# A two-layer encoder with a routed expert stage: the first block's rows picked in turned form, its pass unrolled ahead of the block count

## The chip, the cores and the metric

The kernel runs on one core of a Trainium2 chip. The engines named below are TensorE (PE; its weight loads are listed as PEld), VectorE (DVE), ScalarE (ACT), GpSimd (POOL) and SyncE (SP). The metric is the device time of one execution in microseconds (us).

## What is computed

Two layers over 768 tokens (a sequence of 512 and one of 256) of width 1024, in float32. Each layer has a mixer, an attention to a memory of 256 rows per sequence, and an expert stage. Cut to what matters here:

```python
def memory_cross_attention(x, mem, wq, wkv, wo):     # 4 heads of 256
    q = x @ wq; k, v = split(mem @ wkv)
    return softmax(q @ k.T / 16) @ v @ wo

def grouped_moe(x, router_w, router_bias, w_gate, w_up, w_down):
    e_idx, gw = route(x, router_w, router_bias)      # 2 of 16 experts for each token
    # tokens sorted by expert, each expert's list padded to blocks of 128
    for each block b, expert e:
        h = silu(xb @ w_gate[e]) * (xb @ w_up[e])    # 128 x 512
        yb = h @ w_down[e]                           # 128 x 1024
    y[token] = sum over its 2 slots of gw * yp[slot]

def trunk(x, mem, weights):
    for l in range(2):
        x = layer_norm(ALPHA * x + parallel_mixer(x, ...))
        x = layer_norm(ALPHA * x + memory_cross_attention(x, ...))
        x = layer_norm(ALPHA * x + grouped_moe(x, ...))
```

## The kernel before

Tokens lie in six chunks of 128 (`x[:, c, :]`). A product that must be exact to float32 is made of three faster ones: each operand is split into a high part (ScalarE copies it to the fast type: `split`, `high`, `split_part`) and a low part (VectorE subtracts: `low_weights`, `low`, `low_part`), and `three` (line 2078) multiplies high by high, high by low and low by high. Each engine's program is written out by hand in order; semaphores tie them.

**Memory attention.** Twelve items (a chunk and a pair of heads). For item i TensorE computes scores (`cross_scores`, L2362) two items ahead, ScalarE takes the exponential (L1147), VectorE normalises (`cross_norm`, L1691 and L1694), TensorE turns the result (`turn4`, L2094), ScalarE copies it back (L1164), and after every fourth item TensorE multiplies by the values (L2408). Between these stand the splits of the output weights wx0 to wx3. ScalarE splits wx1 in its turn i = 3, between the copy of item 2 and the exponential of item 4. VectorE's loop stands so: `cross_norm(i)`, `cross_max(i + 2)`, then `low_weights("wx1")` at i = 2.

**Router.** `ROUTER_ORDER` lists TensorE's work: `x3` turns a chunk, `rl` makes its logits (L2424), `rk` the ranks of tokens inside their experts (L2475 to L2480), `wx` output products of the attention, `b0` the first block. VectorE's `choose` finds the experts, `place` the slots and, for the first block, one-hot matrices `pick[c]` (L1794): row t of chunk c has a one in the column of its slot. `b0` multiplies `pick[c]` by the chunk, two products of 512 columns for each chunk (L2447), summed over six chunks in banks 5 and 6. ScalarE copies the two banks to `first_x` (L866), `turn_block(first_x)` turns them in eight transposes (L2493), ScalarE makes the high part (L1223), VectorE the low part (`low_block_xT(0)`, L1807).

**Block table.** After `place(2)` VectorE computes the table of blocks (L1844 to L1864): which expert each of 29 blocks belongs to, where its token list lies, and the number of blocks. The last copy (L1864) raises `ids_ready`. Every engine then reads the number of blocks (`value_load`) and enters its loop. GpSimd waits for `ids_ready` too before it loads the token list of block 1 (L782) and gathers its rows (L785).

**Expert block** (TensorE): gate products (24 of 512 columns, L2517), up products in two halves (L2527), two transposes of h (L2533, after VectorE's `hl_done`), the eight transposes of the next block's rows (`turn_block(xb)`, L2493, after the gather), two more of h (L2542), eight down products (L2553). VectorE multiplies h (L1922, L1924), makes the next rows' low part and the low parts of the next gate and up weights (`low_part`, L1802). Before its loop VectorE makes the low parts 0 to 3 of the first block's weights, finds every token's slots and weights (L1871 to L1902) and, in the first layer, the low part of the next layer's first weights (`low_weights("kvg")`, L1359).

```python
cross_norm(i)
if i + 2 < 12: cross_max(i + 2)
if i == 2: low_weights("wx1")
```

## Time and profile before

| | us |
|---|---|
| median of 3 runs | 2361.14 |
| lowest and highest | 2359.64, 2363.04 |
| the profiled execution | 2357.11 |
| its span, first to last instruction | 2355.3 |
| TensorE, VectorE, ScalarE, GpSimd busy | 2208.6, 1323.8, 992.5, 198.4 |
| mean granted clock of TensorE | 0.963 of full |

The profiled execution is 4.03 us below the median and 1.8 us above its span. The chain that ended last lies on TensorE for 79% of the span, on VectorE for 11% and on ScalarE for 6%. TensorE is the engine to keep fed: a change pays where TensorE stands idle or works at the lower of its two clocks, and hardly elsewhere.

### The profile page before, as it was taken

The page shows a single profiled execution, that of the slowest core. Times are in us where ns is not written, and L with a number is a line of the kernel's source. Part 1 is how long each engine was busy: PE and PEld are TensorE (multiplying, and loading weights), DVE is VectorE, ACT ScalarE, POOL GpSimd, SP SyncE. Part 2 cuts the span into 40 slices and gives each one's busy share as a digit, 9 for nine tenths or more (in the row PEclk, how much of TensorE's full clock was granted, in tenths as well). Part 3 has the DMA queues.
Part 4 walks back from the last instruction along what each step waited for, and adds up shares of the span by engine and source line. Part 5 has one row for each costly group of instructions (what it writes and reads, how often), then busy time and mean ns, then how long its engine had stood idle before and what let it go on. Part 6 is the DMA issues. An engine that isn't in the chain of part 4 may idle for free.

```text
span 2355.3 us, 35471 instructions
## 1 busy us (share of the span) xinstructions
PE 2208.6 (94%) x13292; PEld 1853.1 (79%) x13292; DVE 1323.8 (56%) x2101; ACT 992.5 (42%) x1648; POOL 198.4 (8%) x236
## 2 busy tenths in 40 slices
PE   8899988999999899999889989899999989999997
PEld 7788866989889677777687887598988877777774
DVE  2775377542244766556867636846214556656667
ACT  3354475123232355555235536622323224555553
POOL 0000011000000331000100000100000022200004
PEclk9899998999999899999899999999999989999999
DMA  4145111131110599999511112023211038999996
GB/s 154 45 162 175 37 72 55 55 110 70 55 45 28 192 377 372 382 376 359 199 50 36 37 36 90 10 82 108 86 41 55 37 146 303 378 378 375 383 377 223
DMA packets 78404, 385.64 MB, mean 164 GB/s; under 512 B 10456, under 2 KB 11848, under 8 KB 43464
## 3 DMA queue, kind: packets, MB, share of 16 engines
q1 hardware_dynamic: 55120, 327.83, 37.3%
q0 software_dynamic: 10096, 30.38, 3.6%
q10 hardware_dynamic: 13064, 25.75, 3.0%
q8 instruction: 81, 1.33, 0.2%
q14 instruction: 43, 0.35, 0.0%
HBM read 352.79 MB, written 46.07 MB: 169 GB/s over the span
## 4 chain that ended last, share of the span: by engine, by line
PE 79%; DVE 11%; ACT 6%; issue 2%; DMA 1%; POOL 0%; DVEq 0%; ACTq 0%; SPq 0%
PE bank L2078 39%; PE bank L2553 10%; PE bank L2527 9%; PE bank L2517 8%; PE bank L2228 2%; PE bank L2408 2%; PE bank L2094 2%; ACT x_transposed L1045 1%; PE bank L2362 1%; PE bank L2218 1%; PE bank L2245 1%; PE bank L2493 1%; DVE weight_slots_parts L1361 1%; ACT weight_slots_parts L904 1%; ACT scratch L1003 1%
## 5 line engine op out<-in xcount | busy, mean ns | idle before, releaser
L2078 PE MATMUL bank<-weight_slots_parts,x_transposed_parts 128*128 128x256 f32 x2496 | 475.8, 292 | 13.9 <-ACT mixer_region L968 13.9
L2078 PEld LDWEIGHTS bank<-weight_slots_parts,x_transposed_parts 128*128 128x128 f32 x2496 | 404.9, 200 | 15.2 <-ACT mixer_region L968 15.2
L1802 DVE TENSOR_TENSOR weight_slots_parts<-weight_slots,mixer_region_parts 128x2048 fp32r<-128x2048 f32 x140 | 321.5, 2315 | 85.9 <-ACT mixer_region_parts L1190 85.8
L1190 ACT ACTIVATE mixer_region_parts<-weight_slots 128x2048 fp32r<-128x2048 f32 x140 | 261.0, 1909 | 25.2 <-ACT x_transposed L1265 18.1
L2078 PE MATMUL bank<-x_transposed_parts,weight_slots_parts 128*128 128x512 f32 (+1 forms) x1024 | 263.9, 345 | 0.0
L1361 DVE TENSOR_TENSOR weight_slots_parts<-weight_slots,weight_slots_parts 128x2048 fp32r<-128x2048 f32 x58 | 132.9, 2292 | 231.5 <-ACT weight_slots_parts L904 231.0
L2553 PE MATMUL bank<-weight_slots,x_transposed 128*128 128x512 f32 x560 | 246.4, 593 | 0.0
L2527 PE MATMUL bank<-mixer_region_parts,x_transposed_parts 128*128 128x256 f32 x1120 | 207.3, 283 | 0.1
L2517 PE MATMUL bank<-mixer_region_parts,x_transposed_parts 128*128 128x512 f32 x560 | 194.3, 418 | 4.9 <-DVE x_transposed_parts L1807 4.9
L2078 PEld LDWEIGHTS bank<-x_transposed_parts,weight_slots_parts 128*128 128x128 f32 x1024 | 181.3, 194 | 22.3 <-issue 0.7
L2553 PEld LDWEIGHTS bank<-weight_slots,x_transposed 128*128 128x128 f32 x560 | 103.4, 190 | 117.9 <-issue 101.7
L2078 PE MATMUL bank<-weight_slots_parts,mixer_region_parts 128*128 128x256 f32 x1056 | 181.5, 291 | 4.8 <-DVE mixer_region_parts L1333 4.8
L2527 PEld LDWEIGHTS bank<-mixer_region_parts,x_transposed_parts 128*128 128x128 f32 x1120 | 176.9, 192 | 2.8 <-DVE weight_slots_parts L1802 1.5
L2078 PE MATMUL bank<-weight_slots_parts,x_parts 128*128 128x256 f32 x576 | 167.0, 290 | 0.0
L2078 PEld LDWEIGHTS bank<-weight_slots_parts,mixer_region_parts 128*128 128x128 f32 x1056 | 155.0, 200 | 5.4 <-DVE weight_slots_parts L1361 5.2
L2527 PE MATMUL bank<-weight_slots_parts,x_transposed_parts 128*128 128x256 f32 x560 | 158.4, 283 | 0.0
L2078 PE MATMUL bank<-mixer_region_parts,weight_slots_parts 128*128 128x512 f32 x512 | 137.3, 389 | 0.0
L2517 PEld LDWEIGHTS bank<-mixer_region_parts,x_transposed_parts 128*128 128x128 f32 x560 | 106.6, 190 | 35.2 <-issue 13.2
L904 ACT ACTIVATE weight_slots_parts<-weight_slots 128x2048 fp32r<-128x2048 f32 x58 | 111.0, 1914 | 53.9 <-DMA weight_slots<-in_wkv_mem 31.6
L2078 PEld LDWEIGHTS bank<-weight_slots_parts,x_parts 128*128 128x128 f32 x576 | 114.7, 199 | 0.0
L2078 PEld LDWEIGHTS bank<-mixer_region_parts,weight_slots_parts 128*128 128x128 f32 x512 | 96.0, 188 | 19.6
L2517 PE MATMUL bank<-weight_slots_parts,x_transposed_parts 128*128 128x512 f32 x280 | 110.7, 395 | 0.0
(308 smaller groups left out, 3605.0 us busy)
## 6 DMA issues: line engine op xcount, KB each, us to landing
weight_slots<-in_w_gate SPq DMA_DIRECT2D x70, 1024.0 KB, 7.3
weight_slots<-in_w_up SPq DMA_DIRECT2D x70, 1024.0 KB, 7.0
weight_slots<-in_w_down SPq DMA_DIRECT2D x70, 1024.0 KB, 8.0
weight_slots<-in_w_in SPq DMA_DIRECT2D x20, 1024.0 KB, 5.0
slots_y<-x_transposed ACTq DMA_DIRECT2D x66, 256.0 KB, 7.2
weight_slots<-in_wkv_mem SPq DMA_DIRECT2D x16, 1024.0 KB, 4.9
slots_y<-in_consts SPq DMA_DIRECT2D x6, 2304.0 KB, 17.8
weight_slots<-in_w_out SPq DMA_DIRECT2D x8, 1024.0 KB, 4.8
```

What stands on the lines that cost most here:

```text
L904: nc.scalar.activation(half_hi(name), half_raw(name), ACT.Copy).then_inc(w_hi, 1)
L1003: nc.scalar.activation(probs[:, j, 0:nk], probs[:, j, 0:nk], ACT.Exp, bias=st[:, 4 + j:5 + j], accum_out=st[:, 8 + j:9 + j])
L1190: nc.scalar.activation(hi, raw, ACT.Copy).then_inc(moe.high_ready, 1)
L1361: v.tensor_tensor(half_lo(name), half_raw(name), half_hi(name).bitcast(F32), ALU.subtract).then_inc(w_lo, 1)
L1802: v.tensor_tensor(lo, raw, hi.bitcast(F32), ALU.subtract).then_inc(moe.low_ready, 1)
L2078: ins = pe.matmul(ps, lhs[i](k), rhs[j](k), start=k == 0 and a == 0, stop=k == ks - 1 and a == 2)
L2094: ins = pe.transpose(ps[:, k * P:(k + 1) * P], source(k), ident)
L2228: done(pe.matmul(ps[:, 0:nb * P], qT[hp, j, c * P:(c + 1) * P], kT[hp, k0 * P:(k0 + nb) * P], start=True, stop=True), key)
L2408: ins = pe.matmul(ps[:, jj * 256:(jj + 1) * 256], vm[:, SEQ_OF[2 * cp] * MC + k, j * P:(j + 1) * P], xpt[:, j // 2, k, :], start=(k == 0), ...
L2517: ins = pe.matmul(banks[2][:, :], x_[:, 4 * h + k, :], w_[:, k, :], start=h == 0 and k == 0 and a == 0, stop=h == 1 and k == 3 and a == 2)
L2527: ins = pe.matmul(banks[bank][:, 0:256], x_[:, k, :], w_[:, k, :], start=k == 0 and a == 0, stop=k == KD - 1 and a == 2)
L2553: ins = pe.matmul(banks[5 + h][:, :], hbT[:, k, :], parts[4 + h][0][:, k, :], start=(k == 0), stop=(k == 3))
```

## The change

1. The first block's rows are formed already turned. `b0` now takes 128 columns of x as the stationary operand and `pick[c]` as the moving one: eight products of 128 columns for each chunk. Since eight groups of columns are summed in two banks, two products of zeros (one row, 512 columns) clear the banks first; GpSimd writes the row of zeros. The copies to `first_x` and its eight transposes are gone; ScalarE makes the high part out of the banks.
2. `b0` is spread otherwise in `ROUTER_ORDER`: chunks (0, 1), (2, 3), (4, 5) in place of (0, 1, 2), (3, 4), (5).
3. The first block's pass is written out ahead of the loop and of reading the block count on TensorE and VectorE. VectorE's `low_first_xT` stands in the middle of the block table; `low_part(2, 3)` stands behind the table; the slots and weights (L1871 to L1902) and `low_weights("kvg")` are spread over the first block or stand behind it.
4. `low_weights("wx1")` in the memory attention moves from i = 2 to i = 3.

```diff
-                ("x3", 4, 0), ("x3", 4, 1), ("rl", 1), ("rk", 0), ("wx", 5, 1), ("rk", 1), ("b0", (0, 1, 2)), ("x3", 5, 0), ("x3", 5, 1),
-                ("rl", 2), ("b0", (3, 4)), ("rk", 2), ("b0", (5,))])
+                ("x3", 4, 0), ("x3", 4, 1), ("rl", 1), ("rk", 0), ("wx", 5, 1), ("rk", 1), ("b0", (0, 1)), ("x3", 5, 0), ("x3", 5, 1),
+                ("rl", 2), ("b0", (2, 3)), ("rk", 2), ("b0", (4, 5))])
...
                         if c == 0:
-                            pool.wait_ge(moe.xT_filled, 2)
+                            tile_filled(pool, ("b0", 1))
...
                     for h in range(2):
-                        drain_copy(("b0", h), first_x[:, 512 * h:512 * h + 512], 512)
+                        tile_filled(act, ("b0", h))
+                        nc.scalar.activation(xbT_hi[:, 4 * h:4 * h + 4, :], bank_of(("b0", h))[:, :].rearrange("p (k t) -> p k t", k=4),
+                                             ACT.Copy).then_inc(moe.xT_high_ready, 1)
+                        own(moe.xT_high_ready)
-                    act.wait_ge(moe.xT_filled, 2)
-                    block_xT()
...
-                        if i == 2:
+                        if i == 3:
                             low_weights("wx1")
...
+                    def low_first_xT():
+                        for h in range(2):
+                            dve.wait_ge(moe.xT_high_ready, h + 1)
+                            v.tensor_tensor(xbT_lo[:, 4 * h:4 * h + 4, :], bank_of(("b0", h))[:, :].rearrange("p (k t) -> p k t", k=4),
+                                            xbT_hi[:, 4 * h:4 * h + 4, :].bitcast(F32),
+                                            ALU.subtract).then_inc((drain_sem(("b0", 0)), moe.xT_ready)[h], 1)
...
                     low_part(1, 2)
-                    low_part(2, 3)
                     choose(2)
                     place(2)
...
                     v.tensor_reduce(r_be, cmp_, AX.X, ALU.add)
+                    low_first_xT()
...
                     v.tensor_copy(r_nbi, r_end[:, NE - 1:NE]).then_inc(ids_ready, 1)
-                    low_block_xT(0)
+                    low_part(2, 3)
                     low_part(3, 4)
...
                         v.tensor_tensor(hb[:, 0:256], gact[:, 0:256], banks[3][:, 0:256], ALU.mult).then_inc(moe.hl_done, 1)
+                        if first:
+                            own_weights()
...
+                            if first:
+                                routed_weights(0)
                             low_block_xT(b + 1)
+                            if first:
+                                routed_weights(1)
                             low_part(0, 4 * b + 5)
+                            if first:
+                                late_slots()
                             low_part(1, 4 * b + 6)
...
-                    with dve.Fori(0, n_blocks - 1) as b:
+                    own_slots()
+                    expert_block(0, False, first=True)
+                    late_rows()
...
+                    if l < DEPTH - 1:
+                        now[0] = l + 1
+                        low_weights("kvg")
+                        now[0] = l
+                    n_blocks = dve.value_load(r_nbi[0:1, 0:1], min_val=NE, max_val=BLOCKS)
+                    with dve.Fori(1, n_blocks - 1) as b:
...
+                                pe.wait_ge(zeros_made, l + 1)
+                                for h in range(2):
+                                    pe.matmul(first_ps[h][:, :], zeros[:, 0:P], zeros, start=True, stop=False)
                             for c in key[1]:
                                 pe.wait_ge(picks_ready, 6 * l + c + 1)
-                                for h in range(2):
-                                    ins = pe.matmul(first_ps[h][:, :], pick[c], x[:, c, 512 * h:512 * h + 512],
-                                                    start=c == 0, stop=c == NC - 1)
+                                for k in range(KD):
+                                    h, q = divmod(k, 4)
+                                    ins = pe.matmul(first_ps[h][:, q * P:q * P + P], x[:, c, k * P:k * P + P], pick[c],
+                                                    start=False, stop=c == NC - 1 and q == 3)
...
-                    turn_block(first_x)
-                    pe.wait_ge(ids_ready, 1 * l + 1)
-                    n_blocks = pe.value_load(r_nbi[0:1, 0:1], min_val=NE, max_val=BLOCKS)
...
-                    with pe.Fori(0, n_blocks - 1) as b:
+                    expert_block(0, False)
+                    pe.wait_ge(ids_ready, 1 * l + 1)
+                    n_blocks = pe.value_load(r_nbi[0:1, 0:1], min_val=NE, max_val=BLOCKS)
+                    with pe.Fori(1, n_blocks - 1) as b:
```

The order of instructions, place by place. First, VectorE in the memory attention of the first layer, from the maximum of item 4 on. Before (L1684, L1685 are `cross_max`, L1361 is `low_weights`, L1691 and L1694 are `cross_norm`, L1333 starts the low parts behind item 3):

```order
L1684 TENSOR_REDUCE small<-bank 128x2 [waits filled1,cross_probs_ready]
L1685 TENSOR_SCALAR small<-small 128x2 [waits dve_step_done]
L1361 TENSOR_TENSOR weight_slots_parts<-weight_slots,weight_slots_parts 128x2048 [waits weights_high_part_ready,cross_max_ready]
L1691 RECIPROCAL small<-small 128x2 [waits drained0,weights_low_part_ready]
L1694 TENSOR_SCALAR mixer_region<-mixer_region,small 128x256 [waits dve_step_done]
L1694 TENSOR_SCALAR mixer_region<-mixer_region,small 128x256
L1684 TENSOR_REDUCE small<-bank 128x2 [waits filled2,cross_probs_ready]
L1685 TENSOR_SCALAR small<-small 128x2 [waits dve_step_done]
```

After (the same lines are now four further down: L1688, L1689, L1365, L1695, L1698):

```order
L1688 TENSOR_REDUCE small<-bank 128x2 [waits filled1,cross_probs_ready]
L1689 TENSOR_SCALAR small<-small 128x2 [waits dve_step_done]
L1695 RECIPROCAL small<-small 128x2 [waits drained0,cross_max_ready]
L1698 TENSOR_SCALAR mixer_region<-mixer_region,small 128x256 [waits dve_step_done]
L1698 TENSOR_SCALAR mixer_region<-mixer_region,small 128x256
L1688 TENSOR_REDUCE small<-bank 128x2 [waits filled2,cross_probs_ready]
L1689 TENSOR_SCALAR small<-small 128x2 [waits dve_step_done]
L1365 TENSOR_TENSOR weight_slots_parts<-weight_slots,weight_slots_parts 128x2048 [waits weights_high_part_ready,cross_max_ready]
```

The weights' low part, which waits for ScalarE's split, has moved behind the normalisation of item 3 and the maximum of item 5.

Second, VectorE from the middle of the block table to the first block's last low weights. Before (L1807 is `low_block_xT(0)`, L1802 `low_part(3, 4)`):

```order
L1856 TENSOR_REDUCE mixed<-mixed 128x29 [waits dve_step_done]
L1857 TENSOR_TENSOR mixed<-mixed 128x464
L1858 TENSOR_SCALAR mixed<-mixed 128x29 [waits dve_step_done]
L1859 TENSOR_REDUCE mixed<-mixed 128x29
L1860 TENSOR_TENSOR mixed<-constants,mixed 128x29 [waits dve_step_done]
L1861 TENSOR_SCALAR mixed<-mixed 128x29 [waits dve_step_done]
L1862 CAST mixed<-mixed 128x29 [waits dve_step_done]
L1863 SCALAR_TENSOR_TENSOR mixed<-mixed 128x29
L1864 CAST mixed<-mixed 128x1
L1807 TENSOR_TENSOR x_transposed_parts<-bank,x_transposed_parts 128x512 [waits xT_high_ready_0,block_experts_ready]
L1807 TENSOR_TENSOR x_transposed_parts<-bank,x_transposed_parts 128x512 [waits xT_high_ready_0]
L1802 TENSOR_TENSOR weight_slots_parts<-weight_slots,mixer_region_parts 128x2048 [waits high_ready_0]
```

After (L1811 is `low_first_xT`, L1806 `low_part(2, 3)` and `low_part(3, 4)`):

```order
L1866 TENSOR_REDUCE mixed<-mixed 128x29 [waits dve_step_done]
L1811 TENSOR_TENSOR x_transposed_parts<-bank,x_transposed_parts 128x512 [waits xT_high_ready_0] x2
L1868 TENSOR_TENSOR mixed<-mixed 128x464
L1869 TENSOR_SCALAR mixed<-mixed 128x29 [waits dve_step_done]
L1870 TENSOR_REDUCE mixed<-mixed 128x29
L1871 TENSOR_TENSOR mixed<-constants,mixed 128x29 [waits dve_step_done]
L1872 TENSOR_SCALAR mixed<-mixed 128x29 [waits dve_step_done]
L1873 CAST mixed<-mixed 128x29 [waits dve_step_done]
L1874 SCALAR_TENSOR_TENSOR mixed<-mixed 128x29
L1875 CAST mixed<-mixed 128x1
L1806 TENSOR_TENSOR weight_slots_parts<-weight_slots,mixer_region_parts 128x2048 [waits high_ready_0,block_experts_ready]
L1806 TENSOR_TENSOR weight_slots_parts<-weight_slots,mixer_region_parts 128x2048 [waits high_ready_0]
```

The rows' low part has moved ahead of the last eight instructions of the table, and one more low part of weights stands behind the table.

Third, VectorE between the first block and the second, in the first layer, after the change (L1806 are the second block's last low weights, L1919 and L1922 `late_rows`, L1363 `low_weights("kvg")`, L1935 the second block's h):

```order
L1806 TENSOR_TENSOR weight_slots_parts<-weight_slots,mixer_region_parts 128x2048 [waits high_ready_0] x2
L1919 TENSOR_SCALAR mixed<-mixed 128x128 x3
L1922 TENSOR_SCALAR mixed<-constants,mixed 128x128 x3
L1363 TENSOR_TENSOR mixer_region_parts<-mixer_region,mixer_region_parts 128x2176 [waits xT_ready_0,weights_high_part_ready]
L1975 TENSOR_LOAD mixed [waits weights_low_part_ready]
L1975 ISA x2
L1976 UNCONDITIONAL_BRANCH
L1976 ISA
L1934 REGISTER_ALU [waits g_ready_0]
L1935 TENSOR_TENSOR x_transposed<-x_transposed,bank 128x256 [waits ul_filled_0]
```

Before, the rows from `late_rows` to the branch stood ahead of the first block's h; now they stand ahead of the second's.

## Rows read from the trace of the kernel before

**Rows 1.** The page: the gate products' group (busy us, mean ns | idle before, releaser).

```profile
L2517 PE MATMUL bank<-mixer_region_parts,x_transposed_parts 128*128 128x512 f32 x560 | 194.3, 418 | 4.9 <-DVE x_transposed_parts L1807 4.9
```

**Rows 2.** Chain that ended last, memory attention, first layer: start us, us, what.

```profile
650.80 1.92 ACT weight_slots_parts L904
...
652.81 2.30 DVE weight_slots_parts L1361
...
656.01 0.65 PE bank L2094 x4
...
657.46 8.78 PE bank L2408 x32
```

**Rows 3.** Timeline of TensorE, memory attention: start, us, what [idle before <-releaser].

```profile
698.61 7.18 PE L2408 MATMUL bank<-mixer_region,mixed 128*128 128x256 f32 x32
...
1789.25 0.66 PE L2094 MATMUL bank<-constants,mixer_region 128*128 128x128 f32 x4 [4.21 <-DVE mixer_region L1694]
```

**Rows 4.** Timelines of ScalarE and VectorE there, first layer.

```profile
653.71 0.19 ACT L1147 ACTIVATION_READ_ACCUMULATOR mixer_region<-bank,small 128x1 f32 x1
...
644.72 0.17 DVE L1685 TENSOR_SCALAR small<-small 128x2 f32<-128x2 f32 x1
```

**Rows 5.** Timeline of TensorE, router to first block, first layer.

```profile
791.31 5.42 PE L2447 MATMUL bank<-x,mixed 128*128 128x512 f32 x12 [0.43 <-DVE x L1625]
...
800.41 5.38 PE L2447 MATMUL bank<-x,mixed 128*128 128x512 f32 x8
806.43 0.40 PE L2475 MATMUL bank<-mixed,constants 128*128 128x16 f32 x2 [0.65 <-issue]
...
809.31 2.43 PE L2447 MATMUL bank<-x,mixed 128*128 128x512 f32 x4 [1.81 <-DVE mixed L1794]
...
816.20 0.50 PE L2517 MATMUL bank<-mixer_region_parts,x_transposed_parts 128*128 128x512 f32 x1 [2.60 <-DVE x_transposed_parts L1807]
```

**Rows 6.** TensorE: a run of narrow products; weight loads of L2447 (ns min/median/max).

```profile
383.73 3.51 PE L2285 MATMUL bank<-mixer_region 128*128 128x129 f32 x30
...
L2447 PEld LDWEIGHTS bank<-x,mixed x48: 186/190/337, 791.3 to 1943.6; 128*128 128x128 f32 x48
```

**Rows 7.** Timelines of VectorE and ScalarE, router to first block, first layer.

```profile
800.46 2.29 DVE L1802 TENSOR_TENSOR weight_slots_parts<-weight_slots,mixer_region_parts 128x2048 fp32r<-128x2048 f32 x1 [1.07 <-ACT mixer_region_parts L1190]
...
811.81 0.64 DVE L1856 TENSOR_REDUCE mixed<-mixed 128x29 f32<-128x464 f32 x1
...
814.60 1.29 DVE L1807 TENSOR_TENSOR x_transposed_parts<-bank,x_transposed_parts 128x512 fp32r<-128x512 f32 x2
...
813.70 1.23 ACT L1223 ACTIVATE x_transposed_parts<-bank 128x512 fp32r<-128x512 f32 x2 [1.26 <-PE bank L2493]
```

**Rows 8.** A stretch of TensorE: us, busy (count), granted clock; its gate products (chain).

```profile
800.00:804.00 4.00, 4.00 (x11) 0.57 0.92 309
...
816.20 7.35 PE bank L2517 x24
...
837.54 5.47 PE bank L2517 x24
```

**Rows 9.** GpSimd: block 2's token list, behind block 1's rows; all gathers' landing.

```profile
825.72 0.58 POOL L782 DMA_DIRECT2D block_tokens<-slot_tokens  x1 [5.14 <-issue]
...
DMA to landing us min/median/max: 4.3/6.3/7.0
```

**Rows 10.** VectorE around the first two blocks; VectorE's queue (ns); the chain.

```profile
824.11 0.86 DVE L1899 TENSOR_SCALAR mixed<-mixed 128x128 f32<-128x128 f32 x3
...
825.47 2.42 DVE L1359 TENSOR_TENSOR mixer_region_parts<-mixer_region,mixer_region_parts 128x2176 fp32r<-128x2176 f32 x1
...
840.08 4.73 DVE L1802 TENSOR_TENSOR weight_slots_parts<-weight_slots,mixer_region_parts 128x2048 fp32r<-128x2048 f32 x2
...
L1904 DVEq TENSOR_LOAD <-mixed x1: 553/553/553, 824.1 to 824.1; - x1
...
848.77 0.22 PE bank L2533 x2
```

More of the change, by code:

```diff
@@ L501, in build_program @@
         pick = [y_t[:, 2560 + c * P:2560 + c * P + P] for c in range(NC)]
-        first_x = y_t[:, 3584:4608]
+        zeros = y_t[0:1, 3584:4096]
         slot_numbers = y_t[:, 3328:3456]
@@ L1911, in add_stored, with late_rows @@
+                    def late_rows():
+                        for c in range(NSPREAD):
+                            v.tensor_scalar(spread_rows[c], slot_numbers, r_last_slot[:, c:c + 1], gw[:, NC + c:NC + c + 1],
+                                            ALU.is_equal, ALU.mult).then_inc(spread_made, 1)
+                        for c in range(NSPREAD, NC):
+                            v.tensor_scalar(late_scale[c], ident, gw[:, NC + c:NC + c + 1], None, ALU.mult).then_inc(spread_made, 1)
                     def add_stored(i):
@@ L1917, in add_stored, with expert_block @@
                         dve.wait_ge(combined, 9 * l + i + 1)
-                    def expert_block(b, last):
+                    def expert_block(b, last, first=False):
                         dve.wait_ge(moe.g_ready, b + 2)
```

81 lines of the change are left out of this document (40 added, 41 removed).

## The prediction, made before the changed kernel was run

> **What bounds the kernel now.** I read the page first. TensorE is busy for 2208.6 of 2355.3 us (its first part, in the table), so time can only come from its idle stretches, and from stretches at the lower of its two clocks. Next I followed the chain of waits through the two places that the diff touches. In the memory attention the chain leaves TensorE for ScalarE's split of wx1 and VectorE's low part of it, and comes back after 4.21 us of idle time [rows 2, 3]. At the start of the experts it leaves TensorE for VectorE: TensorE stands idle for 2.60 us before the first gate product [rows 5], and over both layers these products waited 4.9 us [rows 1]. After that product the chain stays on TensorE. So an earlier start of block 0 is kept, unless a later block finds its data late.
>
> **Memory attention: low_weights("wx1") one step later.** In the first layer the maximum of item 4 is over on VectorE at 644.89 [rows 4]. The normalisation of item 3 stands next in need of its exponential alone, which ScalarE has ahead of the split. But VectorE first waits for ScalarE's split (650.80 to 652.72) and then makes the low part (652.81 to 655.11); only then come the normalisation and, at 656.01, the turn on TensorE [rows 2]. From 655.11 to 656.01 is 0.90, so after the change the result is there at 645.8, and TensorE turns item 3 when it is free: at 656.01 - 4.21 = 651.80, ready by 652.45. What is late next is ScalarE's copy of item 3, which still stands behind the split and the exponential of item 4; that ends at 653.90 [rows 4]. From the turn to the products by the values took 657.46 - 656.66 = 0.80 [rows 2]. After: 653.90 + 0.80 = 654.70 against 657.46, a gain of 2.8 us. VectorE now makes the low part after the maximum of item 5, from about 652.9 to 655.2, while TensorE works on these products; wx1 is needed two items later. The second layer shows the same 4.21 [rows 3]. Sum: **5.6 us gained**. On top there may be clock: behind this wait the products took 8.78 us [rows 2], where the same 32 of the next group took 7.18 [rows 3]: 1.6 us that I put down to the lower clock of 1.2 GHz, since nothing else differs. TensorE will still stand idle for 654.70 - 652.45 = 2.25 us. The nearest wait is the one of 2.60 before the experts [rows 5]; I take it that a wait of nearly this length still brings the lower clock: 0 here, and I keep 3.2 us (2 x 1.6) for the range.
>
> **The products of the first block.** Before: 4 instructions of 512 columns for each chunk, (5.42 - 0.59) / 11 = 0.43 us apart (each lasts 0.59) [rows 5], 1.7 us for a chunk. After: 16 instructions of 128 columns. The nearest row has 129 columns, other weights for each, 30 in 3.51 us [rows 6], that is 0.11 to 0.12 apart: 1.8 us for a chunk. The zeros cost four instructions of 512 columns, 4 x 0.43 = 1.7 us; that they have one row only makes them no cheaper that I can see in the columns. They are bounded by 0 and, at half the clock, 3.4. But one chunk fewer stands ahead of the turn of chunk 5, so this part ends at 791.31 + 1.7 + 3.6 = 796.6 against 796.4 before. GpSimd's row of zeros is written long before. The zeros are thus hidden by the chunk that was moved; without that cover they would cost 1.7.
>
> **VectorE's choice of chunk 5.** It began when low_part(2) ended, 800.46 + 2.29 = 802.75 [rows 7]; now it begins when the logits are copied, about 0.2 us behind 800.41 + 0.2, at 801.0. That is 1.8 us sooner, and before it ended when TensorE began the ranks, at 806.43, after an idle 0.65 [rows 5]: now at 804.7. But TensorE is not free by then. Its two chunks begin at 800.6 and the clock there fell to the lower level (0.57 over 800 to 804 [rows 8]). At 1.2 GHz an instruction takes 0.21, so 3.3 us hold 15 and the other 17 take 1.9: end at 805.8. The ranks begin 0.65 sooner, no more. With the full clock they would begin 1.7 sooner.
>
> **The start of the first block.** From the ranks on VectorE has a fixed chain: the last place, then the table. Before, the low part of the rows began at 814.60, behind the whole table, and took 1.29 [rows 7]. Now it begins behind L1856, which ended at 811.81 + 0.64 = 812.45; 0.65 sooner that is 811.8, and the end 813.1. The rows must be there by then: chunk 4's products run while VectorE makes the last pick, chunk 5's from 809.31 - 0.65 = 808.7 to 810.5; ScalarE's two copies of 0.6 [rows 7] end at about 811.7. They make it with 0.1 us to spare for the first half and 0.7 for the second. TensorE began 816.20 - (814.60 + 1.29) = 0.3 after the low part [rows 5, 7]; now at 813.3 or 813.4: **2.85 us in each layer, 5.7 in both**. Bounds: 2.15 (only the rest of the table, 814.60 - 812.45) and 3.9 (the full clock in the paragraph above). The copies to first_x and the eight transposes lay inside VectorE's table and give nothing by themselves. The 24 gate products behind the wait took 7.35 us, and 5.47 in the next block [rows 8]: 1.9 that I put down to the lower clock as well. The new wait, from chunk 5's end at 810.5 to 813.3, is no shorter; I leave them at 7.35 and keep the 1.9 for the range.
>
> **What is pushed back.** The table ends 1.3 - 0.65 = 0.65 later, at 815.2. Low parts 2 and 3 follow until 819.8; the up products need them at 820.7 and 823.6, hidden. The slots and weights are cut into pieces of about 1 us that stand in block 0 where VectorE waits for TensorE or ScalarE; VectorE is busy for 56% of the span, so I take 0, and at most 1 us in each layer. GpSimd gathers block 1 later by 0.65 while TensorE comes 2.85 sooner. Before, the gather was issued at 820.6 and the rows were there about 0.7 before the next token list, at 825.0 [rows 9]; the turn came at 829.4. After: 825.7 against 826.5. It holds by 0.8 us, both layers. Behind block 0, VectorE's low weights end at 840.08 + 4.73 = 844.81 [rows 10] and its h of block 1 must be ready when TensorE reaches the transposes at 848.77 [rows 10]. In the first layer now stand between them: late_rows, 825.47 - 824.11 = 1.36; kvg 2.42; and reading the block count, which must wait for kvg: 0.55 [rows 10], with its checks 0.95; plus 0.3 into the loop and 0.42 for h, estimates from the gaps and lengths of the same instructions before. 844.81 + 1.36 + 2.42 + 0.95 + 0.3 + 0.42 = 850.3, against 848.8: **1.6 us lost, first layer only** (bounds 1.0 and 2.8). In the second layer there is no kvg, h is ready at 847.5, nothing lost. TensorE's own reading of the block count stands behind block 0 now; down products are queued on the engine then, so I take 0; the bound is VectorE's 0.95 in each layer.
>
> **Sum.** 5.6 + 5.7 - 1.6 = 9.7 us. Against the profiled 2357.1 that is 2347.4; against the median of the runs, 2361.1, which is 4.0 above the profiled one, it is **2351.4**.
>
> **Rivals.** (A) *The clock comes back.* The idle time at the values' products shrinks and block 0's wait is filled otherwise; if the lower clock leaves both places, 3.2 and up to 3.8 us more are gained, say 5: 2346.4. For it: less idle time ahead of each; against: waits of this size had the lower clock behind them. (B) *The gather of block 1 takes the place of the wait.* Token list and rows are now moved while the first weight loads run, which begin as much sooner as TensorE does. This gather landed about 4.4 us after it was issued; over all of them it is 4.3 to 7.0, median 6.3 [rows 9]. At 2.6 us more for the rows, and as much for the token list ahead of them, less the slack of 0.8, 4.4 is lost in each layer: 2351.4 + 8.8 = 2360.2. At the median for the rows alone 1.9 - 0.8 = 1.1 in each: 2353.6, inside the forecast's own range. (C) *The narrow products are dear,* the one that ends slower. For it: the weights now change with every product. If a load could not hide behind the product before, each instruction would take 0.19 [rows 6] + 0.11 = 0.30, a chunk 4.8 us. TensorE would start block 0 at 791.31 + 1.7 + 4.0 + 1.1 + 1.7 + 6 x 4.8 = 828.6 (six chunks, the turn and logits between, the ranks, the copy and the low part), 12.4 later than 816.2. 2 x 12.4 - 5.6 + 1.6 = 20.8 slower: 2382. It decides from 2.8 us a chunk on. The 30 products at 0.12 each speak against it. (D) *Block 0's start does not move*: something else on VectorE's path, such as ScalarE's copies, is late: 5.6 - 1.6 gained, 2357.1.
>
> In a stream of narrow products the row of 30 gives 0.12 us for 129 columns, and 0.43 for 512. The Trainium skill (TensorE: Matmul & The Clock Gate, section "Back-to-back issue gap") says that load and product together set the spacing, 81 ns at 128 columns and 131 at 512. That ratio, four times 81 to 131, would make a chunk 4.2 us instead of 1.7, and block 0 8.8 us later in each layer: an estimate from that page is 2375. The row here does not agree, its four narrow products cost 0.47 against 0.43; I go by the row.
>
> **Chances.** As forecast, with the small terms free: 0.62, own range 2348 to 2355. A 0.14. B, its dear end, 0.10. D 0.08, C 0.03, the rest 0.03 on either side. A measurement of this kernel can tell about 0.2%, 4.7 us, from no change; the edge is 2356.4. Faster by more: 0.62 + 0.14 + half of D and half of the rest, 0.82; within it B and the other half of D, 0.14; slower C and a little, 0.04. The range leaves out C, B and the far end of A: 2344.5 to 2357.5.
>
> **What would show it.** In the memory attention TensorE's idle time before item 3's turn gone and about 2.2 us before the values' products in its place, in both layers. 16 narrow products in 1.8 us at full clock. VectorE's low part of the rows right behind L1866, and the first gate product 2.8 us sooner behind the ranks' start less 0.65. In the first layer alone an idle 1.6 us before block 1's transposes of h, put down to VectorE. No wait for the gather before the next rows' transposes in block 0. The prediction is wrong if narrow products are over 0.15 us apart, if the gate products wait for ScalarE, or if the gather is late by more than a microsecond.

## The result, and the profile after

| | before | after |
|---|---|---|
| median of the runs, us | 2361.14 (17 runs, 2356.75 to 2372.67) | 2373.18 (17 runs, 2365.57 to 2379.92) |
| ratio, 95% interval | | 1.0036 [1.0025, 1.0048] |
| the profiled execution, its span | 2357.11, 2355.3 | 2371.34, 2369.7 |
| TensorE busy, mean granted clock | 2208.6, 0.963 | 2216.0, 0.960 |

The forecast was 2351.4 us, a gain; the change costs 0.36%, some 8.5 us. Of the rivals, B names the main cause. It priced it at 8.8 us for both layers; the block in which it lies became 14.8 us longer.

Waits of TensorE in the changed kernel, longest in total (engine, line, releaser: us in total, times, longest). L2526 is `turn_block`, L2548 the first gate products:

```profile
PE bank L2526 <- DMA x_transposed<-x_rows,block_tokens: 13.6, 2, 8.8
...
PE bank L2548 <- DVE x_transposed_parts L1811: 4.7, 2, 2.3
```

The first row is new: the transposes of block 1's rows wait for the gather, 8.8 us in the first layer and 4.9 in the second. The second row answers to [rows 1]: the gate products wait 4.7 us where they waited 4.9.

TensorE's timeline from the first block's products to block 1 (start, us, what, [idle before <-releaser]), first layer, and one row of the second. L2477 are the zeros, L2482 the narrow products, L2510 the ranks, L2558 up, L2564 transposes of h, L2584 down products:

```profile
790.46 1.98 PE L2477 MATMUL bank<-mixed 1*128 1x512 f32 x4 [0.43 <-DVE x L1629]
792.36 5.47 PE L2482 MATMUL bank<-mixed,x 128*128 128x128 f32 x32
...
801.51 5.44 PE L2482 MATMUL bank<-mixed,x 128*128 128x128 f32 x32
806.79 0.29 PE L2510 MATMUL bank<-mixed,constants 128*128 128x16 f32 x2
...
807.61 4.02 PE L2482 MATMUL bank<-mixed,x 128*128 128x128 f32 x32
813.95 0.50 PE L2548 MATMUL bank<-mixer_region_parts,x_transposed_parts 128*128 128x512 f32 x1 [2.33 <-DVE x_transposed_parts L1811]
...
819.51 0.28 PE L2558 MATMUL bank<-mixer_region_parts,x_transposed_parts 128*128 128x256 f32 x1
...
825.27 0.38 PE L2564 MATMUL bank<-constants,x_transposed 128*128 128x128 f32 x2
...
834.41 1.97 PE L2526 MATMUL bank<-constants,x_transposed 128*128 128x128 f32 x8 [8.76 <-DMA x_transposed<-x_rows,block_tokens]
...
836.60 8.82 PE L2584 MATMUL bank<-weight_slots,x_transposed 128*128 128x512 f32 x16
...
858.16 0.44 PE L2564 MATMUL bank<-constants,x_transposed 128*128 128x128 f32 x2 [1.51 <-DVE x_transposed L1935]
...
1970.62 1.97 PE L2526 MATMUL bank<-constants,x_transposed 128*128 128x128 f32 x8 [4.85 <-DMA x_transposed<-x_rows,block_tokens]
```

GpSimd and SyncE's queue there. L786 is block 1's token list, L789 the gather of its rows; L686 and L689 are the loads of block 1's gate and up weights, two of 1 MB each:

```profile
818.20 0.59 POOL L786 DMA_DIRECT2D block_tokens<-slot_tokens  x1 [5.89 <-issue]
825.18 1.00 POOL L789 DMA_INDIRECT x_transposed<-x_rows,block_tokens  x1 [6.40 <-issue]
...
818.21 1.99 SPq L686 DMA_DIRECT2D weight_slots<-in_w_gate  x2
822.58 3.35 SPq L689 DMA_DIRECT2D weight_slots<-in_w_up  x2
```

The list and the first load go out in the same moment. The same two groups in the view of the transfers (KB each, us to landing), 817 to 834:

```profile
block_tokens<-slot_tokens POOLq DMA_DIRECT2D x1, 8.0 KB, 6.2
x_transposed<-x_rows,block_tokens POOLq DMA_INDIRECT x1, 9.2
```

Before, these landed in 2.0 and 4.9 us: the list went out at 816.74, the gather at 819.57, and the first load only at 820.75:

```profile
816.74 0.59 POOL L782 DMA_DIRECT2D block_tokens<-slot_tokens  x1 [4.69 <-issue]
819.57 1.01 POOL L785 DMA_INDIRECT x_transposed<-x_rows,block_tokens  x1 [2.24 <-issue]
820.75 3.32 SPq L685 DMA_DIRECT2D weight_slots<-in_w_gate  x2
```

In the memory attention the item is turned without a wait, and the values' products come after 2.39 us, at the full clock (7.26 us; before 8.78 [rows 2]):

```profile
653.62 7.26 PE L2439 MATMUL bank<-mixer_region,mixed 128*128 128x256 f32 x32 [2.39 <-issue]
```

**Where the time went**, from starts on TensorE in the two profiled executions (after less before, us):

| stretch | layer 1 | layer 2 |
|---|---|---|
| scores before item 3's turn, to item 4's turn | -4.3 | -4.3 |
| item 4's turn to the first block's products | +4.5 | +1.3 |
| these to the first gate product | -1.4 | -1.3 |
| to block 1's gate products | +10.1 | +4.7 |
| block 1 and 2 | +1.7 | +1.0 |

That is +12.0. From the last down product to the end it is +4.0, the rest -1.6; the spans differ by 14.4. The 4.0 come with and without the change: one instruction of VectorE near the end (L1928) took 6.27 us where it took 2.32 before, but 5.61 in the kernel before with a late token list and 2.32 in the changed kernel with its first hold (both below). Without it the pair differs by 10.4, near the measured ratio.

### The profile page after: what moved, and what is told of

Its sections match the earlier page's. It is cut to its first block and busy times, and to the rows that moved or that the text cites. A ratio compares the mean times of both kernels' runs of the same rounds, so it can differ in the third digit from the quotient of the medians.

```text
span 2369.7 us, 35717 instructions
## 1 busy us (share of the span) xinstructions
PE 2216.0 (94%) x13428; PEld 1872.9 (79%) x13428; DVE 1327.1 (56%) x2101; ACT 990.0 (42%) x1644; POOL 190.6 (8%) x238
## 5 line engine op out<-in xcount | busy, mean ns | idle before, releaser
L2109 PEld LDWEIGHTS bank<-weight_slots_parts,x_transposed_parts 128*128 128x128 f32 x2496 | 404.5, 199 | 15.3 <-ACT mixer_region L972 15.1
L1806 DVE TENSOR_TENSOR weight_slots_parts<-weight_slots,mixer_region_parts 128x2048 fp32r<-128x2048 f32 x140 | 322.9, 2327 | 82.7 <-ACT mixer_region_parts L1194 82.5
L1365 DVE TENSOR_TENSOR weight_slots_parts<-weight_slots,weight_slots_parts 128x2048 fp32r<-128x2048 f32 x58 | 132.9, 2292 | 215.5 <-ACT weight_slots_parts L908 214.9
L2584 PE MATMUL bank<-weight_slots,x_transposed 128*128 128x512 f32 x560 | 248.4, 597 | 0.0
L2558 PE MATMUL bank<-mixer_region_parts,x_transposed_parts 128*128 128x256 f32 x1120 | 207.5, 283 | 1.0 <-DVE weight_slots_parts L1806 0.8
L2584 PEld LDWEIGHTS bank<-weight_slots,x_transposed 128*128 128x128 f32 x560 | 104.6, 192 | 118.9 <-issue 103.7
L2548 PE MATMUL bank<-mixer_region_parts,x_transposed_parts 128*128 128x512 f32 x560 | 191.9, 414 | 4.7 <-DVE x_transposed_parts L1811 4.7
L2558 PEld LDWEIGHTS bank<-mixer_region_parts,x_transposed_parts 128*128 128x128 f32 x1120 | 176.9, 192 | 4.4 <-DVE weight_slots_parts L1806 3.3
L2558 PE MATMUL bank<-weight_slots_parts,x_transposed_parts 128*128 128x256 f32 x560 | 158.4, 283 | 0.0
L2548 PEld LDWEIGHTS bank<-mixer_region_parts,x_transposed_parts 128*128 128x128 f32 x560 | 105.2, 188 | 33.8 <-issue 7.4
L2548 PE MATMUL bank<-weight_slots_parts,x_transposed_parts 128*128 128x512 f32 x280 | 109.5, 391 | 0.0
```

The costliest lines, as they stand in the source:

```text
L1365: v.tensor_tensor(half_lo(name), half_raw(name), half_hi(name).bitcast(F32), ALU.subtract).then_inc(w_lo, 1)
L1806: v.tensor_tensor(lo, raw, hi.bitcast(F32), ALU.subtract).then_inc(moe.low_ready, 1)
L2109: ins = pe.matmul(ps, lhs[i](k), rhs[j](k), start=k == 0 and a == 0, stop=k == ks - 1 and a == 2)
L2548: ins = pe.matmul(banks[2][:, :], x_[:, 4 * h + k, :], w_[:, k, :], start=h == 0 and k == 0 and a == 0, stop=h == 1 and k == 3 and a == 2)
L2558: ins = pe.matmul(banks[bank][:, 0:256], x_[:, k, :], w_[:, k, :], start=k == 0 and a == 0, stop=k == KD - 1 and a == 2)
L2584: ins = pe.matmul(banks[5 + h][:, :], hbT[:, k, :], parts[4 + h][0][:, k, :], start=(k == 0), stop=(k == 3))
```

## Experiments

All were timed beside the kernel before. "The wait for the rows" is TensorE's idle time before `turn_block` of block 1, in the first and the second layer.

**Is it the wx1 edit?** `wx1_only` is the kernel before with

```diff
-                        if i == 2:
+                        if i == 3:
                             low_weights("wx1")
```

> The kernel before with one edit: the low part of wx1 in the memory attention one item later. Both traces show that the edit saves 4.3 us there in each layer in the changed kernel (2.8 of waiting, 1.5 of lower clock), and that the stretch from item 4's turn to the first ranks (the same instructions, the same idle times) took 4.5 and 1.3 us longer there, at a lower granted clock. Theory G (the lower clock is only moved: a wait filled in the attention brings the lower clock in the router): the edit alone gives 8.7 less about 5.8, that is 2 to 4 us faster than before, 2357 to 2359, with the logits behind the 1.94 us of idle time at the lower clock again. Theory F (the slower router comes from the rest of the change): the full 8.7, 2352.

Measured: 2359.3, ratio 0.9988 [0.9973, 1.0004]. `no_wx1` is the changed kernel without it:

> The changed kernel with the low part of wx1 back in its old place. Theory G: what the edit brought is about 3 us net, so this is some 3 us slower than the changed kernel, 2375 to 2377, and the router stretch takes 121.7 us as before. Theory F: 8.7 us slower, 2382. In both, the wait of 8.8 and 4.9 us for block 1's rows stays: it has nothing to do with this edit.

Measured: 2368.1, ratio 1.0034 [1.0010, 1.0058]: not slower than the changed kernel. The attention did what it should in every kernel with the edit: 2.39 us of idle time, then 7.26 us. What differs is the stretch behind it, from item 4's turn to the first block's products, the same instructions with the same idle times in all kernels. In the profiled executions, both layers of each, it took 122.7, 122.7, 122.7, 124.3, 124.5 and 121.2 us in the three kernels with the old place (before, `no_wx1`, `late_list`), mean 123.0; in the eleven with the new place 122.8 once, 124.0 to 124.4 twelve times and 126.9 to 127.2 nine times, mean 125.3. The difference lies in the granted clock. The windows of the logits that wait 1.94 us for ScalarE in both (us, busy, clock, DMA, GB/s), before and then after:

```profile
767.80:769.80 2.00, 1.93 (x17) 0.99 0.24 96
```

```profile
762.60:766.20 3.60, 3.51 (x17) 0.50 0.36 146
```

The 16 products took 1.93 us before and 3.57 after, and the output products behind them 8.55 in place of 7.49. The attention, for its part, gained more than the first pair shows. From the scores before item 3's turn to item 4's turn it took 14.4 us in all 22 layers with the new place; with the old place it took 18.7 in three layers of six and 20.1 or 20.2 in the other three (one in `no_wx1`, two in `late_list`), where the values' products took 10.2 us. So on average 5.0 us are gained in the attention, and 2.2 of them are given back as lower clock (1.2 GHz) in the router. The time of `wx1_only` fits theory G and leaves out theory F's 8.7 us. G's other price, `no_wx1` some 3 us slower than the changed kernel, did not come.

In `no_wx1` the wait for the rows was 0.96 and 0.72 us, where "8.8 and 4.9 stay" was expected: a miss. Its timelines say why. The 24 gate products ran partly at the lower clock (7.2 us to the first up product; 5.6 in the changed kernel), and SyncE's first load waits for half of them. It was issued 0.2 us behind the twelfth and 0.6 us behind the token list, which landed in 2.6 us.

In the changed kernel these products no longer hold the load. The twelfth ended at 816.96, and the load went out only at 818.21, when SyncE had read the table, whose last instruction is this one on VectorE:

```profile
815.87 0.15 DVE L1875 CAST mixed<-mixed 128x1 int32<-128x1 f32 x1
```

The list went out 2.2 us behind it (1.9 in the second layer), the load 2.2 (1.5). Before the change the load went out 6.2 and 5.9 us behind the table, right behind the twelfth gate product. So one instruction now releases both transfers. TensorE's clock adds to it: in `no_wx1`, at the lower clock, the gate products still held the load back, to 2.7 us behind the table in both layers.

**Is it the collision?** `hold_list` and `hold_rows` are the changed kernel with one wait ahead of SyncE's loop, for the value 1 (list landed) and 2 (rows landed); `hold_up` waits for the list there and for the rows ahead of the up weights alone:

```diff
                     n_blocks = sp.value_load(r_nbi[0:1, 0:1], min_val=NE, max_val=BLOCKS)
+                    sp.wait_ge(moe.gather_turn, 1)
```

> The changed kernel, where SyncE starts the loads of block 1's weights only once the token list of block 1 has landed (one wait on a constant ahead of its loop). Theory T (the token list, 8 KB, is issued in the same moment as the first two loads of 1 MB and lands 6.4 us later in place of 2.2, and the rows then share the DMA engines with the next two loads): the list lands in 2.2 us again, the gather is issued at 821 in place of 825.2, the first load at 821 too, as before the change. TensorE's wait for the rows falls from 8.8 and 4.9 us to 0 to 2 in each layer, the down products behind it run at the full clock: 10 to 14 us faster than the changed kernel, 2359 to 2363. Rival U (the gather is late because GpSimd itself or the block table is late): the wait shrinks by less than 2 us, 2371.

Measured: 2366.8, ratio 1.0016 [1.0003, 1.0030]; waits for the rows 4.05 and 4.33. GpSimd (L787 list, L790 gather) and SyncE:

```profile
816.46 0.59 POOL L787 DMA_DIRECT2D block_tokens<-slot_tokens  x1 [5.88 <-issue]
819.25 1.00 POOL L790 DMA_INDIRECT x_transposed<-x_rows,block_tokens  x1 [2.21 <-issue]
...
819.81 0.98 SPq L686 DMA_DIRECT2D weight_slots<-in_w_gate  x2
```

The list landed in 2.0 us again, as expected. But the rows, issued 0.56 us before the first load, took 8.7.

> The changed kernel, where SyncE starts the loads of block 1's weights only when block 1's rows have landed. With the first hold (list only) the rows still took 8.7 us, beside 4 MB of loads that had all become due. Theory T (what is small and urgent loses against loads of 1 MB that are issued beside it): the rows take about 4 us, landing by 823.5, TensorE's wait for them is gone in both layers; 3 MB of weights start 4 to 5 us later than in the changed kernel and are needed from 837 on. If their slack holds, 2357 to 2360; if it does not, TensorE waits 1 to 4 us for the low parts of block 1's gate weights, 2361 to 2366. Rival U (the gather takes 8 us whatever else moves): no gain against the first hold, 2367.

Measured: 2366.8, ratio 1.0004 [0.9986, 1.0023]. With nothing beside them the rows took 4.3 and 4.6 us (TensorE still waited 1.2 us for them in the first layer):

```profile
x_transposed<-x_rows,block_tokens POOLq DMA_INDIRECT x1, 4.3
```

But list and rows, one behind the other, took 10 to 12 us from the table's end, so the loads came 9 to 10 us later against the first gate product than in the changed kernel, not 4 to 5, and TensorE then waited for weights, 3.7 us in sum in the first layer and 2.05 in the second.

> As the run before, but only the up and down weights of block 1 wait for its rows; its gate weights wait for the token list alone. Theory T: the rows share the DMA engines with 2 MB in place of 4 and land after 6 us, as before the change (819.6 to 825.7): TensorE's wait is 0 to 1 us in each layer, no weights are late; 2357 to 2361. Rival U: as the first hold, 2367.

Measured: 2370.0, ratio 1.0026 [1.0008, 1.0043]; rows 8.6 and 8.2 us, waits 4.0 and 3.3. A miss: halving the traffic beside the gather did nothing. The gather was issued 0.2 and 0.6 us after the first load.

**The table first.** `table_first` moves `low_first_xT` behind the whole table, its place before the change; `table_kvg` also moves `low_weights("kvg")` ahead of block 0:

```diff
                     v.tensor_reduce(r_be, cmp_, AX.X, ALU.add)
-                    low_first_xT()
...
                     own(ids_ready)
+                    low_first_xT()
```

> The changed kernel with the low part of the first block's rows behind the whole table, as before the change; the rest of it stays. The table ends 1.3 us sooner, TensorE starts the first block 1.3 us later. Theory T: the list is issued about 1 us ahead of the first loads and lands in 2 to 4 us, the gather is issued by 821; the wait for the rows falls to between 1 and 4 us in each layer, 5 to 10 us faster than the changed kernel in sum, 2363 to 2368. Rival U (it is the earlier start of TensorE, not the order of the transfers): the wait shrinks only by the 1.3 that TensorE comes later, and the time stays at 2373.

Measured: 2361.4, ratio 0.9993 [0.9978, 1.0008]: better than expected, no wait for the rows. The gate products had 4.57 us of idle time ahead of them and ran at the lower clock, so TensorE came to the turn at 825.65, 1.9 us after the rows had landed. These still took 7.7 us. VectorE, GpSimd and SyncE:

```profile
812.37 4.48 DVE L1806 TENSOR_TENSOR weight_slots_parts<-weight_slots,mixer_region_parts 128x2048 fp32r<-128x2048 f32 x2
...
816.05 1.68 POOL L789 DMA_INDIRECT x_transposed<-x_rows,block_tokens  x1 [2.16 <-issue]
...
817.31 3.05 SPq L686 DMA_DIRECT2D weight_slots<-in_w_gate  x2
```

The gather instruction lasts 1.68 us in place of 1.0. It ends 0.88 us after VectorE's low parts (816.85), and 0.42 us behind the first load.

> The kernel with the whole table first (2361.4), and also the low part of kvg and with it nothing else back ahead of the first block. The idle 2.2 us before block 1's transposes of h in the first layer goes; VectorE makes the first block's h up to 2.4 us later if it has no slack there. Expected if it has: 2359. If it has not: 2361 again, with an idle 1 to 2 us before the first block's transposes of h.

Measured: 2361.9, ratio 0.9999 [0.9982, 1.0016]: the idle time at h is gone from the profile (0.44 us came elsewhere), the time is the same within the interval.

**Order or traffic?** Over all profiles the landings of the rows fall into two groups by one number, the end of the gather instruction less the issue of the first weight load. Up to -0.16 they take at most 5.2 us, from +0.26 on 6.0 or more; within the second group they do not follow it:

| kernel | gather's end less first load, us | rows landed after, us |
|---|---|---|
| `hold_rows` | no load beside it | 4.3, 4.6 |
| before | -0.17, -0.34 | 4.9, 4.6 |
| `wx1_only` | -0.17, -1.02 | 5.0, 4.5 |
| `gather_ahead`, with `_kvg`, layer 1 | -0.16, -0.16 | 5.2, 5.0 |
| the same two, layer 2 | +0.26, +0.27 | 7.1, 7.2 |
| `table_first` | +0.42, +0.41 | 7.7, 7.8 |
| `table_kvg` | +0.47, +0.42 | 7.2, 7.8 |
| `hold_list` | +0.44, +0.87 | 8.7, 9.3 |
| `hold_up` | +1.2, +1.6 | 8.6, 8.2 |
| `no_wx1` | +4.0, +3.1 | 6.5, 7.1 |
| after | +8.0, +7.0 | 9.2, 6.9 |
| `after_again` | +7.8, +7.3 | 8.9, 6.3 |
| `wide_zeros` | +8.0, +7.1 | 8.7, 7.4 |
| `late_list` | +7.9, +7.2 | 6.9, 6.0 |

In `gather_ahead` SyncE starts the loads of block 1 right behind the gather:

```diff
                     n_blocks = sp.value_load(r_nbi[0:1, 0:1], min_val=NE, max_val=BLOCKS)
+                    sp.wait_ge(gather_out, l + 1)
...
                         gather_block()
+                        if isinstance(b, int) and b == 0:
+                            pool.sem_inc(gather_out, 1)
```

> The changed kernel, where SyncE starts block 1's weight loads right behind the gather of its rows (GpSimd raises a semaphore behind the gather instruction). In the runs so far the rows took 4.5 to 5.0 us where the gather instruction ended before the first load was issued (by as little as 0.17 us), and 6.5 to 9.3 us where it ended behind it (by as little as 0.4 us). Theory Q (order in the queues decides, not the amount of traffic): the rows take 4.5 to 5 us, TensorE waits 0 to 1.5 us in each layer and no weights are late; 7 to 10 us faster than the changed kernel, 2360 to 2364. Rival V (traffic beside it decides: all four loads are due by then): 8 to 9 us as with the hold for the list, 2367.

Measured: 2358.8, ratio 0.9978 [0.9966, 0.9989], beside 2371.4 for the changed kernel in the same comparison. GpSimd (L791 the gather), SyncE and TensorE's turn (L2530) in the first layer:

```profile
822.56 1.00 POOL L791 DMA_INDIRECT x_transposed<-x_rows,block_tokens  x1 [3.91 <-issue]
...
823.72 2.04 SPq L687 DMA_DIRECT2D weight_slots<-in_w_gate  x2
...
827.80 1.09 PE L2530 MATMUL bank<-constants,x_transposed 128*128 128x128 f32 x8 [2.30 <-DMA x_transposed<-x_rows,block_tokens]
```

The waits are 2.30 and 2.13 us, above the 0 to 1.5 expected: in the second layer a load still slipped ahead by 0.26 us and the rows took 7.1. Then the time, 2358.8, is even below theory Q's 2360 to 2364. Theory V's 8 to 9 us for the rows came in neither layer.

> The same with the low part of kvg back ahead of the first block: the idle 1.5 to 2.2 us before block 1's transposes of h in the first layer goes. 1 to 2 us faster than without it, 2359 to 2362. If VectorE's slack ahead of the first block's h is not there, the same time.

Measured: 2359.9, ratio 0.9994 [0.9974, 1.0013]. The waits for the rows are 1.53 and 2.21 us. The idle time at h is gone; no gain can be told from its lack. Its interval also includes no change against the kernel before, so the gain of `gather_ahead` over that kernel rests on one comparison; the lead of both over the changed kernel does not.

**The collision alone.** `late_list` is the kernel before, with nothing of the change, but a late token list:

```diff
                     n_blocks = pool.value_load(r_nbi[0:1, 0:1], min_val=NE, max_val=BLOCKS)
+                    pool.wait_ge(moe.ga_done, 1)
                     load_tokens(slice(1, 2))
```

> The kernel before, where GpSimd issues block 1's token list only when TensorE has done half of the first block's gate products; this is the moment at which SyncE issues the first loads of block 1's weights. Nothing else of the change is in it. Theory T (the small transfers lose as soon as 1 MB loads are issued ahead of them): the list is issued at 820.8 in place of 816.7 and lands in 5 to 6 us in place of 2.0, the gather in 7 to 9 in place of 4.9; the rows land near 835, TensorE waits 4 to 7 us in each layer, 2370 to 2378 in sum. Rival U (transfers take as long as ever): list out 4 us later, gather at 823.6, rows at 828.5 before TensorE comes at 829.4: 2361 to 2363, no change.

Measured: 2381.6, ratio 1.0081 [1.0066, 1.0097]. GpSimd (L782, L785), SyncE and TensorE's turn:

```profile
828.52 0.59 POOL L782 DMA_DIRECT2D block_tokens<-slot_tokens  x1 [10.11 <-issue]
833.58 1.69 POOL L785 DMA_INDIRECT x_transposed<-x_rows,block_tokens  x1 [4.47 <-issue]
...
827.39 3.07 SPq L685 DMA_DIRECT2D weight_slots<-in_w_gate  x2
...
840.52 1.74 PE L2494 MATMUL bank<-constants,x_transposed 128*128 128x128 f32 x7 [4.61 <-DMA x_transposed<-x_rows,block_tokens]
```

List 4.2 and 4.3 us, rows 6.9 and 6.0, waits 4.6 and 3.8: one wait on the list brings the collision into the kernel before. But the time lies above the 2370 to 2378 expected. In the profile, 22.8 us longer than the one before, the first block became 6.4 and 5.3 us longer. Another 6.4 us stand ahead of the first layer's first block, where the edit does nothing (3.2 of them in the attention and the router, at a lower clock); what brings the rest was not found.

**The changed kernel once more.**

> The changed kernel once more, beside these on the same chip. Expected 1.0025 to 1.0048 of the kernel before again. Where its first block's gate products run at the full clock (5.7 us) the first loads and the token list go out together and the wait for the rows is 5 to 9 us; where they run at the lower clock (7.3 us) the list is ahead and the wait is about 1 us.

Measured: 2371.4, ratio 1.0045 [1.0028, 1.0062]; list and first load at 818.51 and 818.53, waits 8.31 and 4.56 us, gate products at the full clock in both layers, as in the first profile.

**The zeros.** In `wide_zeros` they have 128 rows in place of one, the same 512 columns:

```diff
-        zeros = y_t[0:1, 3584:4096]
+        zeros = y_t[:, 3584:4096]
```

> The changed kernel with the zeros made 128 rows high in place of one; the four products of zeros keep their 512 columns. In all eight places of the four kernels that have them, the granted clock fell to 0.50 for about 3.3 us right behind them (the first 32 narrow products took 5.4 us, the last 32 take 4.0), and it never did there without them. Theory H (products of one row load TensorE too little): the clock stays at 1.00 and the 32 products take 4.0 us; the ranks come 1.4 us sooner. Rival (the clock falls for what stands ahead of the zeros): 5.4 us as before. The time depends on the collision behind it and may be anything from 2366 to 2374.

The windows behind the zeros, changed kernel and then `wide_zeros` with a second window at its next 32 products:

```profile
792.40:795.40 3.00, 3.00 (x15) 0.50 1.02 428
```

```profile
788.00:791.00 3.00, 3.00 (x29) 1.00 1.01 425
796.00:801.00 5.00, 5.00 (x25) 0.50 0.62 187
```

The clock behind the zeros stays at 1.00, and 32 products take 3.73 us for 5.47. Theory H held there. But the logits behind them (3.02 us for 1.93) and the next 32 products (5.99 us) ran at the lower clock instead, and the ranks began 16.7 us after the zeros, for 16.3: nothing is gained. Measured: 2365.1, ratio 1.0006 [0.9989, 1.0023], though the profiled execution has the same waits for the rows (8.28, 5.40); with 2368.8 us it was among the slowest of its twelve. How the others went was not profiled, so why this kernel is faster than the changed one stays open.

## Why the prediction was wrong

- **Memory attention.** The waits came nearly as forecast: the turn without idle time, 2.39 us (2.25) before the values' products. I put the clock term at 0 and kept it for the range; it was there, 1.5 us in each layer. What the text did not have at all: the clock that is gained at one place is lost at another. The stretch behind gave 4.5 and 1.3 us back. Over all profiles 5.0 - 2.2 is 2.8 in each layer. That both together are the forecast's 5.6 is luck: two terms of the clock that the sum did not have nearly cancel. `wx1_only` measured 2.8 in all, between 6.4 gained and 0.9 lost.
- **Narrow products.** 0.12 apart, as read from the row of 30: 32 in 4.02 us. Rival C falls, and with it the estimate from the Trainium skill (TensorE: Matmul & The Clock Gate, section "Back-to-back issue gap"). What failed here is the sum "796.6": it took the full clock, and behind the one-row zeros the clock fell, in both layers of all ten kernels that have them (5.3 to 5.5 us each). The first part took 7.2 us for a forecast of 5.3; TensorE's ranks came 16.3 us after the part's start, where 14.5 was forecast and 15.1 was before.
- **Start of block 0.** For that reason 1.4 and 1.3 us in place of 2.85, and the table ended 2.3 us later against the same start, in place of 0.65. The low part of the rows stood where it was said, and TensorE began 0.05 us after it.
- **The gather: "It holds by 0.8 us".** This is the step that decided. The slack was read as arrival less landing, with a landing time that stood still. (It also took the end of the gather's instruction, 820.6, for its issue, 819.57; the rows had landed at 824.43, not 825.0, so the slack was 0.6 us larger than written, and was lost all the same.) But the landing time was short only because the gather's instruction ended 0.17 us before the first weight load was issued, and the change moves both: the table later, TensorE's call for weights sooner. Rival B had the mechanism; its price of 2.6 us each was the longest landing of all gathers less this one's (7.0 - 4.4 [rows 9]). Measured were 4.2 more for the list and 4.3 more for the rows in the first layer, 2.9 and 2.3 in the second. The waits were 8.8 and 4.9 us where the text had none. On top, behind 8.8 us of idle time the turn and the down products ran at the lower clock (8.82 us for 7.09). Nor did I see that the gate products had kept the first load behind the list. Started sooner against the table, and at the full clock, which the text had as a gain of 1.9, half of them ended 0.9 us behind the table; then the load goes out with the list.
- **kvg and the block count.** 1.5 us idle before block 1's transposes of h, first layer alone: 1.6 was forecast.
- **The rest** (slots and weights in pieces, TensorE's own reading of the count) cost nothing, as forecast.

## What to carry to other kernels

When a change lets an engine start sooner, ask what that engine calls for: here its gate products had held the weight loads back, and once they came early, 4 MB met a list of 8 KB and a gather on which the next block hung. For a small transfer that someone waits for, the slack is not the time to its landing but its lead over the next large one, and a wait that lets the large one go second showed no cost here (`gather_ahead`: 12 us less than the changed kernel in the same comparison). Filling an idle stretch of TensorE may only move its lower clock to the next one: credit the wait, not the clock.

## What was not expected of the hardware

- **A lead of 0.2 us decides over 2 us and more.** Rows whose gather ended 0.16 to 1.0 us ahead of the first load landed in 4.5 to 5.2 us; 0.26 to 0.9 us behind it, in 7.1 to 9.3 (1.2 to 8 us behind it, in 6.0 to 9.2); alone, in 4.3 to 4.6. A list of 8 KB took mostly 1.8 to 2.2 us alone and 4.2 to 6.2 where a load went out in the same moment or before it. The Trainium skill (DMA: Bandwidth & Descriptors, section "Queues, rings and completion order") says that each DMA engine takes the queues in turn, a packet from each. An estimate by that rule is that rows beside loads need up to twice their time: 8.6 to 9.2, from 4.3 and 4.6. The traces, with 6.0 to 9.3, agree in size; that a lead of 0.16 us keeps the rows whole the page does not tell.
- **A gather waits for VectorE.** The instruction took 1.0 us in most places, but 1.68 and 1.98 where a low part of 2048 columns ran on VectorE beside it, and then ended 0.88 and 0.86 us behind that (`table_first`). In all profiles together 16 gathers of block rows, of 462, took 1.3 to 2.9 us; all 16 were issued while a low part of 2048 columns (once 2176) ran, and ended 0.85 to 0.93 us behind it. The Trainium skill (Trainium Architecture — The Big Picture, section "What this means for kernel authors") says that these two engines share a port pair under an exclusive lock. The traces agree, and VectorE had it: its low parts kept their 2.28 to 2.29 us (2.42 the one of 2176 columns) beside the gathers that waited.
- **Products of one row bring the lower clock**, though TensorE is busy: four in 1.98 us, then 0.50 for some 3 us; with 128 rows it stayed at 1.00.
- Without any load beside it, the list took 3.5 to 3.7 us in the first layer of `hold_rows`, `hold_up` and the two `gather_ahead`, and 1.8 to 2.0 in their second; this was not explained.
